# Small reorderings in an f32 three-block block kernel on one core: the last scores pair, gate sums over eight banks, squares first, the end's diagonal and a store on ScalarE

## The reference, cut to what matters

```
layer 1: h = rmsnorm(x); x += short_conv(h);  h = rmsnorm(x); x += swiglu(h)
layer 2: h = rmsnorm(x); x += window_attention(h) (16 heads of 64, sinks, alibi)
         h = rmsnorm(x); x += swiglu(h)
layer 3: u = rms_norm(h); proj = u @ w_in -> q, k, v, x_lru, g_lru, gate_attn, gate_lru
         attention on rotated q, k;  xc = conv(x_lru)
         r = sigmoid(xc @ w_rg_a + b);  i = sigmoid(xc @ w_rg_i + b)   # block diagonal
         linear recurrence; two branches, merged, @ w_out
         h += rms_norm(mix); u = rms_norm(h); m = relu(u @ up)^2 @ down
         h += rms_norm(m)
```

## Time and profile before

| | us |
|---|---|
| median of three runs (1003.33 to 1003.53) | 1003.48 |
| the profiled execution | 1004.07 |
| its span, first to last instruction | 1002.1 |
| TensorE busy | 994.6 |
| VectorE busy | 723.6 |
| ScalarE busy | 613.5 |
| GpSimd busy | 261.5 |
| granted TensorE clock, mean over the span (1 is full) | 1.000 |

### The profile page before, as it was taken

How to read it: one execution, slowest core, us unless ns; L and a number is a source line. 1 busy time by engine, 2 the same in 40 slices (tenths; PEclk the granted TensorE clock), 3 DMA queues, 4 the chain that set the end, 5 groups by cost and what they waited for, 6 DMA issues and landing times.

```text
span 1002.1 us, 19205 instructions
## 1 busy us (share of the span) xinstructions
PE 994.6 (99%) x6468; PEld 896.7 (89%) x6468; DVE 723.6 (72%) x1114; ACT 613.5 (61%) x1110; POOL 261.5 (26%) x249
## 2 busy tenths in 40 slices
PE   9999999999999999999999999999999999999998
PEld 7899888889999898888899999899999988888886
DVE  6997777786767678787676787577877768774443
ACT  7555666664556767666654567857485578764332
POOL 2441233221212222222121136402031445441000
PEclk9999999999999999999999999999999999999999
DMA  8775555545553235545455555554444536556531
GB/s 321 255 309 182 182 197 180 198 168 190 200 173 123 85 139 199 203 175 207 159 190 198 175 200 174 175 178 154 168 154 169 187 122 213 203 171 203 175 126 43
DMA packets 37710, 180.90 MB, mean 181 GB/s; under 512 B 3472, under 2 KB 7824, under 8 KB 19984
## 3 DMA queue, kind: packets, MB, share of 16 engines
q1 hardware_dynamic: 37504, 179.99, 51.0%
q10 hardware_dynamic: 144, 0.08, 0.1%
HBM read 179.01 MB, written 1.05 MB: 180 GB/s over the span
## 4 chain that ended last, share of the span: by engine, by line
PE 96%; ACT 2%; DVE 1%; issue 1%; POOL 0%; POOLq 0%; ACTq 0%
PE bank L482 32%; PE bank L488 26%; PE bank L484 10%; PE bank L486 10%; PE bank L526 4%; PE bank L525 4%; PE bank L524 4%; PE bank L605 1%; PE bank L729 1%; PE bank L713 1%; PE bank L743 0%; PE bank L594 0%; PE bank L943 0%; PE bank L612 0%; PE bank L504 0%
## 5 line engine op out<-in xcount | busy, mean ns | idle before, releaser
L1469 DVE TENSOR_TENSOR wlo<-raw,whi 128x1024 fp32r<-128x1024 f32 (+1 forms) x289 | 354.1, 1225 | 83.0 <-ACT whi L976 80.2
L976 ACT ACTIVATE whi<-raw 128x1024 fp32r<-128x1024 f32 (+2 forms) x289 | 301.6, 1044 | 106.6 <-PE bank L488 100.1
L488 PE MATMUL bank<-xa,wlo 128*128 128x256 f32 x1664 | 345.7, 280 | 0.0
L482 PE MATMUL bank<-xa,whi 128*128 128x512 f32 x1056 | 336.4, 396 | 0.5 <-DVE xa L1924 0.5
L488 PEld LDWEIGHTS bank<-xa,wlo 128*128 128x128 f32 x1664 | 296.5, 189 | 42.7
L482 PEld LDWEIGHTS bank<-xa,whi 128*128 128x128 f32 x1056 | 164.2, 189 | 5.6 <-issue 1.0
L484 PE MATMUL bank<-xa,whi 128*128 128x256 f32 x608 | 164.9, 289 | 0.0
L486 PE MATMUL bank<-xa,whi 128*128 128x256 f32 x608 | 160.7, 283 | 0.0
L1007 ACT ACTIVATE spill<-bank 128x256 f32<-128x256 f32 x167 | 63.8, 382 | 137.2 <-PE bank L488 137.2
L484 PEld LDWEIGHTS bank<-xa,whi 128*128 128x128 f32 x608 | 116.3, 191 | 2.2 <-issue 1.9
L486 PEld LDWEIGHTS bank<-xa,whi 128*128 128x128 f32 x608 | 116.4, 191 | 0.3
(11 more groups left out here) (228 smaller groups left out, 1420.4 us busy)
## 6 DMA issues: line engine op xcount, KB each, us to landing
raw<-in_stream SPq DMA_DIRECT2D x137, 1024.0 KB, 4.8
raw<-in_stream SPq DMA_DIRECT2D x42, 512.0 KB, 4.8
raw<-in_stream SPq DMA_DIRECT2D x8, 768.0 KB, 4.3
bias<-in_bias SPq DMA_DIRECT2D x1, 3072.0 KB, 12.9
raw<-in_stream SPq DMA_DIRECT2D x8, 256.0 KB, 5.5
x<-in_x SPq DMA_DIRECT2D x4, 256.0 KB, 5.2
out<-x SPq DMA_DIRECT2D x3, 256.0 KB, 2.5
cons<-in_cons SPq DMA_DIRECT2D x1, 576.0 KB, 8.9
```

The costliest lines, as they stand in the source:

```text
L482: pe.matmul(dst, whi[:, slot, at + i, :], X[:, k, :, :], start=first and i == 0, stop=False)
L488: ins = pe.matmul(narrow, wlo[:, slot, at + i, :], X[:, k, 0, :], start=False, stop=last and i == len(tiles) - 1)
L976: act.activation(whi[:, p, 0:kts, :].rearrange("p k m -> p (k m)"), src, ACT.Copy)\
L1469: dve.tensor_tensor(wlo[:, p, 0:kts, :].rearrange("p k m -> p (k m)"), src, whi[:, p, 0:kts, :].rearrange("p k m -> p (k m)").bitcast(F32) ...
```

## The change

It touches the order and the places of work, not what is computed.

1. TensorE issues scores1(7) right behind turn1(5). VectorE runs denominators(6) behind mask1(7).
2. The four parts of rg go to banks 4 and 7, 5 and 6, 0 and 1, 4 and 7. The waits of rg, v2, scores2, turn2 and values2 follow. ScalarE runs the sigmoids of a part ahead of `next_weights`.
3. In out2, ScalarE squares tile 6 ahead of `next_weights`.
4. In mpre, ScalarE squares tiles 6 and 7 directly from PSUM and copies them to SBUF after that.
5. At the end, ScalarE makes the diagonal and issues the store of tiles 4 and 5 itself.
6. GpSimd's `fourth_piece` waits for the counts of the pieces ahead of its own.

```diff
--- before.py
+++ after.py
@@ -362,7 +362,8 @@
 
         def rg_acc(part, m):
 
-            return bank[4 + 2 * (part % 2) + m // 2][:, m % 2 * TOK:(m % 2 + 1) * TOK]
+            banks = ((bank[STAT], bank[OUT]), bank[ATT:ATT + 2], bank[0:2], (bank[STAT], bank[OUT]))[part]
+            return banks[m // 2][:, m % 2 * TOK:(m % 2 + 1) * TOK]
 
         def q_bank(t):
 
@@ -463,8 +464,7 @@
                 for h in range(2):
                     load_half(B0["mdn"] + j, h, chunks[j // 2])
             for done, count, tiles, t in ((final, 1, slice(0, 4), 0), (final, 2, slice(4, 8), 0),
-                                          (final_act, 1, slice(0, 4), 1), (final_act, 2, slice(4, 6), 1),
-                                          (final, 3, slice(6, 8), 1)):
+                                          (final_act, 1, slice(0, 4), 1), (final, 3, slice(6, 8), 1)):
                 sp.wait_ge(done, count)
                 sp.dma_start(out[:, tiles, t * P:(t + 1) * P], x[:, tiles, t * P:(t + 1) * P]).then_inc(stored, 16)
             sp.wait_ge(stored, 16 * 5)
@@ -790,9 +790,9 @@
                     wo_blocks(3, 4, 0)
                 head_sums(s + 7)
             turn1(5)
+            scores1(7)
             wo_blocks(0, 3, 2)
             values1(5)
-            scores1(7)
             wo_blocks(3, 5, 2)
             wo_blocks(4, 5, 0, 1)
             turn1(6)
@@ -830,7 +830,7 @@
                 if i >= 2:
                     pe.wait_ge(masked, h - 1)
                 else:
-                    pe.wait_ge(rg_emptied, 16)
+                    pe.wait_ge(rg_emptied, 8)
                 b = bank[ATT + i % 2]
                 pe.matmul(b[:, 0:P], q2[:, i, 0:P], k2[:, i, 0:P], start=True, stop=True)
                 pe.matmul(b[:, P:3 * P], q2[:, i, P:2 * P], k2[:, i, :], start=True, stop=True)\
@@ -842,7 +842,7 @@
                 if i >= 1:
                     pe.wait_ge(pt_ready, h)
                 else:
-                    pe.wait_ge(rtok_ready, 1)
+                    pe.wait_ge(rg_emptied, 16)
                 for j in range(3):
                     ins = pe.transpose(bank[STAT][:, j * P:(j + 1) * P], pr2[:, i % 2, j * P:(j + 1) * P],
                                        con("ident", P))
@@ -854,6 +854,8 @@
                 pe.wait_ge(emptied, T0["v2"] + (2 if i < 4 else 4))
                 if i >= 1:
                     pe.wait_ge(att_lo, h)
+                else:
+                    pe.wait_ge(rg_emptied, 16)
                 o = bank[OUT]
                 v = [vtok2[:, tb, i * HD2:(i + 1) * HD2] for tb in range(2)]
                 pt = pt2[:, i % 2, :]
@@ -880,9 +882,14 @@
                         pe.wait_ge(xc_lo, 4 * part + 4)
                     if part == 0:
                         pe.wait_ge(rbc_ready, NORM["pre2"] + 1)
+                        pe.wait_ge(lntok_ready, 1)
+                    if part == 1:
                         pe.wait_ge(taps, 3 * KT)
-                    if part >= 2:
-                        pe.wait_ge(rg_emptied, 4 * (part - 1))
+                    if part == 2:
+                        pe.wait_ge(emptied, T0["k2"] + KT)
+                        pe.wait_ge(rot_out, 2 * KT)
+                    if part == 3:
+                        pe.wait_ge(rg_emptied, 4)
                     for m in range(4):
                         t = 4 * (part % 2) + m
                         ins = blocks(r % 4, xb, [t // 2 * 2, t // 2 * 2 + 1], rg_acc(part, m), True, True, at=2 * m)
@@ -892,8 +899,11 @@
 
                     j, p = divmod(r - AT["v2"], 4)
                     if p == 0:
-                        pe.wait_ge(emptied, T0["v2"] + 2 * j - 2)
-                        pe.wait_ge(rot_out, 14 + 2 * j)
+                        if j == 0:
+                            pe.wait_ge(emptied, T0["k2"] + KT - 2)
+                            pe.wait_ge(rot_out, 2 * KT - 2)
+                        else:
+                            pe.wait_ge(rg_emptied, 12)
                     for t in range(2):
                         ins = unit(p, xa, 2 * p, t, ring[2 * j + t], p == 0, p == 3)
                     ins.then_inc(piece_done, 1)
@@ -1326,12 +1336,12 @@
                 n = R0 + r
                 if AT["rg"] <= r < AT["v2"]:
                     part = r - AT["rg"]
-                    next_weights(n)
                     act.wait_ge(piece_done, n + 1)
                     for m in range(4):
                         t = 4 * (part % 2) + m
                         act.activation((rr if part < 2 else ga)[:, t, :], rg_acc(part, m), ACT.Sigmoid,
                                        bias=vec("ba" if part < 2 else "bi", t)).then_inc(rg_emptied, 1)
+                    next_weights(n)
                 else:
                     if r == 0:
                         rms(NORM["pre2"])
@@ -1367,10 +1377,12 @@
                 n = 4 * B0["out2"] + t
                 if t < 7:
                     spill_tile(n, t % 4)
-                    next_weights(n)
-                if t < 7:
+                    if t < 6:
+                        next_weights(n)
                     act.wait_ge(emptied, T0["out2"] + t + 1)
                     square(t, NORM["post2"], mix[:, t, :])
+                    if t == 6:
+                        next_weights(n)
                 else:
                     act.wait_ge(piece_done, n + 1)
                     square(t, NORM["post2"], ring[t % 4][:, 0:TOK])
@@ -1396,15 +1408,18 @@
 
             pre_hi(0)
             pre_hi(1)
-            for t in (0, 2, 4, 6):
+            for t in (0, 2, 4):
                 keep_x(t)
                 keep_x(t + 1)
                 square_x(t)
-                if t < 6:
-                    pre_hi(t + 2)
+                pre_hi(t + 2)
                 square_x(t + 1)
-                if t < 6:
-                    pre_hi(t + 3)
+                pre_hi(t + 3)
+            for t in (6, 7):
+                act.wait_ge(split_lo, SPLIT["mpre"] + t + 1)
+                square(t, NORM["mpre"], new_x(t))
+            keep_x(6)
+            keep_x(7)
 
             def up_hi(tile, slot):
 
@@ -1450,11 +1465,15 @@
                    .then_inc(mln_ready, 1)
                 act.wait_ge(mln_ready, t + 1)
                 act.activation(minv[:, t:t + 1], mln[:, t:t + 1], ACT.Exp, scale=-0.5).then_inc(minv_ready, 1)
+                act.wait_ge(minv_ready, t + 1)
+                act.activation(diag[:, t, :], con("ident", P), ACT.Copy, scale=minv[:, t:t + 1]).then_inc(diag_ready, 1)
             for i, (tiles, b) in enumerate(((slice(0, 4), bank[2]), (slice(4, 6), bank[3]))):
                 act.wait_ge(turned_out, 3 + i)
                 n = tiles.stop - tiles.start
                 act.activation(x[:, tiles, P:2 * P], b[:, 0:n * P].rearrange("p (a b) -> p a b", a=n), ACT.Copy)\
                    .then_inc(final_act, 1)
+            act.wait_ge(final_act, 2)
+            act.dma_start(out[:, 4:6, P:2 * P], x[:, 4:6, P:2 * P]).then_inc(stored, 16)
 
 
         @block.vector
@@ -1750,9 +1769,11 @@
                    .then_inc(att_lo, 1)
 
             for s in range(PAIRS1):
-                if s >= 1:
+                if 1 <= s < PAIRS1 - 1:
                     denominators(s - 1)
                 mask1(s)
+                if s == PAIRS1 - 1:
+                    denominators(s - 1)
                 if s >= 2:
                     out_lo(s - 2)
                 if s < 6:
@@ -1965,9 +1986,6 @@
                    .then_inc(mbase_ready, 1)
             for t in range(2):
                 gained_half(1, t)
-                dve.wait_ge(minv_ready, t + 1)
-                dve.tensor_scalar(diag[:, t, :], con("ident", P), minv[:, t:t + 1], None, ALU.mult)\
-                   .then_inc(diag_ready, 1)
                 if t == 0:
                     for half in range(2):
                         tiles = slice(4 * half, 4 * half + 4)
@@ -2109,10 +2127,12 @@
                 n = 4 * B0["mup"] + 3
                 pool.wait_ge(raw_loaded[1], 16 * B0["mup"] + 16)
                 pool.wait_ge(piece_done, n - 3)
+                pool.wait_ge(hi_ready, n)
                 hi, lo = [w[:, 3, :, :].rearrange("p k m -> p (k m)") for w in (whi, wlo)]
                 src = raw[:, B0["mup"] % 2 * 2 + 1, PIECE:2 * PIECE]
                 pool.tensor_copy(hi, src).then_inc(hi_ready, 1)
                 pool.wait_ge(hi_ready, n + 1)
+                pool.wait_ge(lo_ready, n)
                 pool.tensor_tensor(lo, src, hi.bitcast(F32), ALU.subtract).then_inc(lo_ready, 1)
 
             fourth_piece()
```

## The result

The changed kernel takes 1007.62 us, the median of six runs (1007.30 to 1008.22). Measured beside them, the kernel before took 1003.3 to 1004.8 us. Single slow executions of it far above the rest (1843.16 us here; 3459.57 and 1205.32 us beside later kernels) are left out of every ratio. The ratio is 1.0038, with a 95% interval of 1.0026 to 1.0049, so the change costs 2.6 to 4.9 us. The profiled execution took 1007.30 us with a span of 1005.5, against 1004.07 and 1002.1 before.

The account below looks back on a forecast made before the run. TensorE, busy 994.6 of 1002.1 us, was taken to bound the kernel, so edits count only in its gaps. 3.3 + 0.33 - 0.55 - 0.33 - 0.2 = +2.55 us on the 1003.48 median gave 1006.0 us, range 1004.6 to 1008.1.

Parts of the forecast that it names:

- the clock, a rival: TensorE's clock falls in the gap before turn1(6), 4 us at half speed: +2 us more, 1008.0 us; chance 0.12.
- two signs of being wrong: mask1(7) starting well before exps1(6) ends, or matmuls of double length behind the gap before turn1(6).
- Part 1: Pair 6 attention: denominators(6) behind mask1(7) starts 2.73 us later, GpSimd's scaling slows 0.6 us, delaying turn1(6): +3.3 us.
- So it slides whole: The 4.84 us chain from turn1(6) to turn1(7) all starts from turn1(6), so it moves later unchanged.
- Part 2: Gate sums in new banks: third group stalls 1.04 us for the rotation copy, fourth has no stall: +0.33 us.
- bound of -0.7: Gate sums' lower bound: both stalls gone, if the rotation copy came earlier.
- Part 3: out2: square of tile 6 ahead of the weights lets GpSimd's add and the statistics come sooner: -0.55 us, bounds -0.3 and -0.6.
- Part 4: mpre: squares of the last two tiles from PSUM end TensorE's wait before the statistics: -0.33 us, bounds -0.1 and -0.35.
- Part 5: Kernel end: diagonal on ScalarE nothing within 0.1; other store on ScalarE's queue frees the last store: -0.2 us.
- all stalls of parts 1 and 2 gone too: Low case of the rival that earlier scores help: attention and gate-sum stalls vanish, -2.5 us, 1001.0; a third of chance 0.12.

Follow-up runs that it names:

- the filler: Changed kernel with seven f32 matmuls of 256 columns, result unread, put into TensorE's gap ahead of turn1(6): 1006.90 us, ratio 1.0033.
- the copy-first kernel: Changed kernel with denominators(6) in its old place and ScalarE's two last-k2-tile rotation copies ahead of the first gate-sum sigmoids: 1002.20 us, ratio 0.9984.
- the kernel with the 3.48 us gap: Kernel before with only denominators(6) moved behind mask1(7): 1008.66 us, median of 5, ratio 1.0043.

## Why the prediction was right, and where a step was off

The forecast was 1006.0 us, and the range 1004.6 to 1008.1 holds the measured 1007.62. The direction and the mechanism are as forecast. The sum is 1.2 to 1.6 us too low, and almost all of that is one term. The measured time lies above the forecast's own bounds (at most +3.9 on 1003.48, or 1007.4); the range reached it only because it was stretched to 1008.1 for the clock, a rival with a chance of 0.12. One of the two signs of being wrong that the prediction names did appear: behind the gap matmuls of 256 columns were issued each 0.21 us instead of 0.12.

**Part 1, the wait.** Forecast +3.3 us with bounds 2.7 and 3.5, measured 3.18 between the two transposes. Each step held: mask1(7) held by rq (shown by the kernel that makes rq sooner), denominators(6) behind it, and GpSimd held up by half_rest. Forecast 0.6 us for that last one, measured 0.45, and shown by the kernel that moves half_rest away.

**Part 1, what follows the wait.** "So it slides whole" was the step that failed. From turn1(6) to turn1(7) it is 5.85 us and not 4.84. I had this as a rival, a fallen clock, and gave it 0.12. It is what happened, in every profile with the long gap. The argument against it was that the gap is no longer than the warm-up at the start, and that was no evidence; behind its first matmul the trace before had no idle stretch of TensorE over 0.56 us. With a price of +2 us the rival was sized too high in turn: it took 4 us at half speed, all on the path. The traces show about three microseconds, which lengthened TensorE's own work by 1.27 us in the changed kernel (1.53 and 1.50 us in two others), and TensorE had 0.26 us to spare there. So it cost 1.01 us. That it is the clock, the filler shows.

**Part 2.** Forecast +0.33 us, measured +0.32: v2 starts 12.62 us behind part 0 instead of 12.30. The stall of 1.04 us before part 2 came out as worked out, with the copy ending 0.14 us before the start. Its bound of -0.7 is what the copy-first kernel reached, with -0.78.

**Part 3.** Forecast -0.55, measured -0.53: from the start of out2's last pair of matmuls to the first of mup it is 4.78 us (816.09 - 811.31) instead of 5.31. GpSimd's add at 0.74 us, between VectorE's subtractions, is the reason given, and in the trace VectorE indeed runs nothing beside it (from 809.88 to 811.32). The next limit is the square of tile 7, as forecast: it ends at 812.13 and the second statistics matmul starts at 812.18.

**Part 4.** Forecast -0.33, measured -0.26 from the first mup matmul to the last of w_down (181.61 against 181.87 us). At the statistics it is -0.37. 0.1 us is given back later, which I did not trace to a line. No run undoes part 3 or part 4 by itself. The kernel with denominators(6) back and the gate sums as before, in which of the priced parts only 3, 4 and 5 are left, is 0.77 us faster than the kernel before by the medians, where their measured terms give 0.91, and its interval just reaches no change.

**Part 5.** The diagonal, forecast as nothing within 0.1, costs 0.08 us: ScalarE takes 0.40 us for it and starts 0.03 us behind minv's end, VectorE 0.28. The store, forecast -0.2: the last one is issued 2.51 us behind the last turn-out's start (1002.47 - 999.96), where it was 2.71. These two are read from the traces alone; no timing can tell them.

```profile
1002.02 0.42 DVE L1996 COPY x<-bank 128x256 f32<-128x256 f32 x1 [2.48 <-PE bank L953]
1002.03 0.41 ACTq L1476 DMA_DIRECT2D out<-x  x1
1002.47 0.37 SPq L469 DMA_DIRECT2D out<-x  x1
```

**The sum again**, with measured terms: 3.18 + 1.01 + 0.32 - 0.53 - 0.26 + 0.08 - 0.2 = +3.6 us, inside the interval of the ratio (2.6 to 4.9) and near the 3.4 us by which the spans differ. What is left are starts that differ by some tenths from trace to trace. Two sums in the prediction don't add up, and nothing hangs on either: its bounds give about +0.7 to +3.8 and not +1.0 to +3.9, and with all stalls of parts 1 and 2 gone too it comes to -2.1 us and not -2.5.

## What to carry to other kernels

Before an instruction is moved behind another for the sake of an input that now comes sooner, look for the input that is still late: here the scores came two microseconds sooner, and rq held the same instruction as before. A wait on a path with no cover is paid in full, and a long one can be paid again in TensorE's clock: the three gaps of 2.84 to 3.48 us traced here cost 1.0 to 1.3 us more each, and filling one took that away. When banks are handed round to remove one wait, check which late reader of the new bank takes its place; here two copies of 0.8 us together, moved up in one queue, turned a loss of 0.3 us into a gain of 0.8.

## What the runs showed of the hardware

TensorE's granted clock stayed at 1.00 with 1.69 us idle and fell to 0.50 in the kernels with 2.84, 3.29 and 3.48 us. At 2.84 it fell about 1 us after work had resumed, and at 3.48 also after it, so the next thing to be slowed need not be the one that waited. The price on the path was 1.0 to 1.3 us. No gap between 1.69 and 2.84 us was tried. It seems to vary from run to run: of five executions of the kernel with the 3.48 us gap, one has a mean granted clock of 1.000 and the shortest time (1006.83 us), two have 0.996 and the longest (about 1009.0 us). The Trainium skill, TensorE: Matmul & The Clock Gate, Part 1: The HAM clock gate, says that an idle array falls back to half rate; the traces here agree, with 0.50 granted.

The hold-up between VectorE and GpSimd goes both ways. GpSimd's 1.61 us became 2.06 beside a subtraction of VectorE with two SBUF inputs, and that subtraction became 1.08 instead of 0.68. VectorE's scaling with one SBUF tensor and a scalar is drawn out too: of two beside GpSimd's multiply of 1.08 us, one took 1.07 us. That last case is one trace, and no run takes GpSimd away from beside it.
